# A ring of 19 half places for expert weights, and the final norm's weight spread by identity products

## The reference, cut to what matters

```python
h = h + merged @ w_out[layer]
h = h + hierarchical_moe(rmsnorm(h, norm_ffn_w[layer]), router_group_w[layer], ..., expert_w_gate[layer],
                         expert_w_up[layer], expert_w_down[layer])
out = rmsnorm(h, norm_final_w)
return out[:, N_META:]
```

## Time and profile before

| | |
|---|---|
| time, median of 3 | 776.92 us (776.09 to 777.96) |
| the profiled execution's own time | 777.54 us |
| its span | 775.8 us |
| TensorE busy (matmul) | 748.4 us, 96% |
| TensorE weight load busy | 534.8 us, 69% |
| VectorE, ScalarE, GpSimd busy | 323.0, 312.2, 124.5 us |
| moved by DMA | 241.08 MB, 311 GB/s over the span |
| granted TensorE clock, mean | 0.999 |

### The profile page before, as it was taken

The page is one execution under the profiler, slowest core; times in us unless marked ns, Lnnn a source line. Parts: engine busy times, 40 slices in busy tenths (PEclk is TensorE's granted clock), DMA queues, the critical chain, the costliest instruction groups (busy, mean ns, idle before and its releaser), DMA issues.

```text
span 775.8 us, 16103 instructions
## 1 busy us (share of the span) xinstructions
PE 748.4 (96%) x6517; PEld 534.8 (69%) x6517; DVE 323.0 (42%) x793; ACT 312.2 (40%) x632; POOL 124.5 (16%) x208
## 2 busy tenths in 40 slices
PE   8999999999999999899999999999999999998995
PEld 8989989998999988655555555565555555455452
DVE  5785787688675855812211311221222112112012
ACT  6876678576584744712112121222122121111123
POOL 7373242225433640000000000000000000000000
PEclk9999999999999999999999999999999999999999
DMA  8537555554754458999999999999999999999993
GB/s 206 145 84 179 153 139 143 138 150 111 187 141 124 144 197 307 414 408 422 412 430 427 429 427 426 427 431 424 424 429 427 427 430 426 427 427 427 422 415 125
DMA packets 83554, 241.08 MB, mean 311 GB/s; under 512 B 7185, under 2 KB 65666, under 8 KB 71826
## 3 DMA queue, kind: packets, MB, share of 16 engines
q1 hardware_dynamic: 83170, 239.19, 81.2%
q10 hardware_dynamic: 304, 0.79, 0.3%
HBM read 238.92 MB, written 1.05 MB: 309 GB/s over the span
## 4 chain that ended last, share of the span: by engine, by line
PE 72%; DMA 16%; DVE 5%; issue 3%; POOL 2%; ACT 1%; SPq 1%; DVEq 0%; POOLq 0%; ACTq 0%
PE banks L2154 22%; PE banks L1808 19%; PE banks L2212 11%; DMA ring<-in_expert_w_up_dram 10%; DMA ring<-in_expert_w_down_dram 5%; PE banks L2085 3%; PE banks L2003 2%; PE banks L2167 2%; PE banks L1927 1%; PE banks L1940 1%; PE banks L2188 1%; DVE desk L1381 1%; PE banks L1944 1%; PE banks L1965 1%; PE banks L1988 1%
## 5 line engine op out<-in xcount | busy, mean ns | idle before, releaser
L2154 PE MATMUL banks<-ring,bench 128*64 128x256 f32 x2048 | 239.9, 388 | 7.7 <-DMA ring<-in_expert_w_up_dram 5.6
L2154 PEld LDWEIGHTS banks<-ring,bench 128*64 128x64 f32 x2048 | 145.9, 134 | 108.7 <-issue 20.8
L1808 PE MATMUL banks<-rounded 128*128 128x256 f32 (+3 forms) x1344 | 197.5, 293 | 1.3 <-DVE rounded L1342 0.9
L1808 PEld LDWEIGHTS banks<-rounded 128*128 128x128 f32 (+1 forms) x1344 | 170.1, 187 | 5.3 <-POOL rounded L1206 1.1
L1711 DVE TENSOR_TENSOR bench<-banks,bench 128x256 f32<-128x256 f32 x32 | 13.6, 425 | 259.5 <-PE banks L2154 171.7
L2212 PE MATMUL banks<-ring,bench 128*64 128x512 f32 x512 | 116.9, 598 | 1.4 <-DMA ring<-in_expert_w_down_dram 0.9
L1105 ACT ACTIVATE ysb<-banks 64x512 f32<-64x512 f32 x63 | 37.3, 592 | 148.1 <-PE banks L2212 147.3
L2212 PEld LDWEIGHTS banks<-ring,bench 128*64 128x64 f32 x512 | 34.1, 136 | 64.0 <-issue 60.2
L873 ACT ACTIVATE rounded<-room 128x1024 fp32r<-128x1024 f32 x64 | 67.4, 1054 | 23.5 <-PE banks L1808 15.1
L1094 ACT ACTIVATE bench<-banks 128x256 f32<-128x256 f32 x32 | 12.3, 385 | 146.1 <-PE banks L2188 146.1
L1330 DVE TENSOR_TENSOR rounded<-room,rounded 128x1024 fp32r<-128x1024 f32 x49 | 61.4, 1252 | 16.6 <-ACT rounded L873 15.6
(11 more groups left out here) (309 smaller groups left out, 857.6 us busy)
## 6 DMA issues: line engine op xcount, KB each, us to landing
ring<-in_expert_w_down_dram SPq DMA_DIRECT2D x28, 2048.0 KB, 26.4
ring<-in_expert_w_gate_dram SPq DMA_DIRECT2D x27, 2048.0 KB, 25.2
ring<-in_expert_w_up_dram SPq DMA_DIRECT2D x27, 2048.0 KB, 26.5
room<-in_w_in_dram SPq DMA_DIRECT2D x56, 512.0 KB, 4.2
ring<-in_expert_w_up_dram SPq DMA_DIRECT2D x16, 512.0 KB, 7.0
ring<-in_expert_w_down_dram SPq DMA_DIRECT2D x16, 512.0 KB, 7.0
ring<-in_expert_w_gate_dram SPq DMA_DIRECT2D x12, 512.0 KB, 5.8
room<-in_w_out_dram SPq DMA_DIRECT2D x8, 512.0 KB, 4.3
```

The source lines that it names most:

```text
L1808: ins = T.matmul(o, a, b[:, k, lo_at:L], start=(k == 0 and n == 0), stop=(k == KT - 1 and n == 2))
L2154: ins = T.matmul(pb[5 + c][half * 64:half * 64 + SLOTS, 0:256], xgT[:, q % ROOMS, kt, j * SLOTS:(j + 1) * SLOTS], w[:, kt, half], start=(k ...
```

## The change

1. **Half places.** The ring's 9 places become 18 halves, and all of `spare` becomes a 19th (8 KB a partition each). Half h of chunk n (= 3e+c) goes to half place (2n+h) mod 19. Chunks 0 to 8 stay where they were, as whole loads. From chunk 9, gate of expert 3, each chunk is two loads of 1 MiB, with 8 KB rows: the first waits until the chunk ten before is used up, the second until half of the chunk nine before is (a new semaphore `half`, raised by TensorE in the middle of each chunk). Chunk 9's first half goes to `spare` and waits for the router's logits. `PIECES` keep their sizes. The quartered loads and their semaphore go.
2. **Landing semaphores.** There are ten (`LANDS`) in place of nine, and `landed` counts the loads of a chunk.
3. **The final norm's weight.** The 128-row load of L789 goes. In its place SyncE loads `gain_out`, 32 bytes a partition, right after `gain` at the start. In experts 28 and 29, after `turn_mid`, TensorE does `spread_gain`: 8 products each of a broadcast column of `gain_out` with 64 columns of the identity, into bank 4, and VectorE copies the bank into the new `wfin`, which lies in the second half of `xgT` of room 0 (not used after expert 27).
4. **Counts.** `gain`'s load raises `bias_land` now, so the three waits for it and for the biases become waits for all four loads. The router's count goes from 5 to 4 loads.

```diff
-ROUT = 5 * 16
+ROUT = 4 * 16
-QUARTERED = [(RINGS, 0), (RINGS, 1), (RINGS, 2), (RINGS + 1, 2)]
+HALVES = 19
+LANDS = 10
+GAIN_PARTS = 2
...
+def slot_of(e, c):
+    return (3 * e + c) % LANDS
+
+def loads_of(e, c, again):
+    if (e, c) in PIECES or e == 0 and not again:
+        return 0
+    if 3 * e + c >= HALVES // 2:
+        return 2
+    return QUARTERS if e == 1 and c < 2 and not again else 1
+
+def loads_until(e, c, again):
+    return sum(loads_of(m // 3, m % 3, again) for m in range(slot_of(e, c), 3 * e + c + 1, LANDS))
...
-        wfin = spare[:, D:2 * D]
+        gain_out = sb("gain_out", [P, KT])
...
+        wfin = xgT[:, 0, KT // 2:KT, :].rearrange("p k s -> p (k s)")
...
+        def half_at(e, c, half):
+            at = (2 * (3 * e + c) + half) % HALVES
+            if at == HALVES - 1:
+                return spare[:]
+            return ring[:, RING_AT[at // 2], at % 2 * CHUNK // 2:(at % 2 + 1) * CHUNK // 2]
...
+        def load_half(eng, e, c, half):
+            dst, src = half_at(e, c, half), (gate_v, up_v, down_v)[c][e][:, half * CHUNK // 2:(half + 1) * CHUNK // 2]
             if (e, c) in PIECES:
-                parts = PIECES[e, c]
+                parts = PIECES[e, c] // 2
...
-                eng.dma_start(dst, src).then_inc(S(f"w_land{3 * (e % RINGS) + c}"), 16)
+                eng.dma_start(dst, src).then_inc(S(f"w_land{slot_of(e, c)}"), 16)
...
-            sp.dma_start(gain[:], norm_ffn_w[0].rearrange("(p k) -> p k", k=KT)).then_inc(S("gain_land"), 16)
+            sp.dma_start(gain[:], norm_ffn_w[0].rearrange("(p k) -> p k", k=KT)).then_inc(S("bias_land"), 16)
+            sp.dma_start(gain_out[:], norm_final_w.rearrange("(p k) -> p k", k=KT)).then_inc(S("bias_land"), 16)
...
-                    taken(sp, ("G", HEADS - 1))
-                    sp.dma_start(wfin, norm_final_w[None, :].to_broadcast([P, D])).then_inc(S("rout_land"), 16)
...
                 for e in range(EXPERTS):
-                    for c, used in enumerate(("gate", "up", "y")):
-                        if (e, c) in QUARTERED and not again:
...
-                        if e >= RINGS:
-                            sp.wait_ge(S(used), base + (e - RINGS + 1))
...
+                    for c in range(3):
+                        n = 3 * e + c
+                        if 2 * n + 1 < HALVES:
+                            if again or (e and (e, c) not in EARLY):
+                                load_chunk(sp, e, c)
                             continue
+                        before = n - LANDS
+                        if before >= 0:
+                            sp.wait_ge(S(used[before % 3]), base + before // 3 + 1)
+                        elif not again:
+                            sp.wait_ge(S("logits"), TT)
+                        load_half(sp, e, c, 0)
+                        sp.wait_ge(S("half"), chunks + (before + 2))
+                        load_half(sp, e, c, 1)
...
-                    act.wait_ge(S("bias_land"), 2 * 16)
+                    act.wait_ge(S("bias_land"), 4 * 16)
...
                     if q + 1 < QUADS:
                         bring(q + 1, j)
+                    elif j < GAIN_PARTS:
+                        dve.wait_ge(S("gathered"), parts + QUADS * PARTS + j + 1)
+                        V.tensor_copy(wfin[:, j * 512:(j + 1) * 512], pb[4][:]).then_inc(S("xgT"), 1)
...
+                def spread_gain(n):
+                    pe.wait_ge(S("xgT"), parts + QUADS * PARTS + n - 2)
+                    for k in range(KT):
+                        ins = T.matmul(pb[4].rearrange("p (j k) -> p k j", k=KT)[:, k, :], gain_out[:, k:k + 1].to_broadcast([P, P]),
+                                       ident[:, n * 64:(n + 1) * 64], start=True, stop=True, skip_group_check=True)
+                    ins.then_inc(S("gathered"), 1)
...
                             ins = T.matmul(pb[5 + c][...], xgT[:, q % ROOMS, kt, j * SLOTS:(j + 1) * SLOTS],
-                                           w[:, kt, half], ...)
-                        if first and (kt + 1) % (KT // QUARTERS) == 0 and kt < KT - 1:
-                            ins.then_inc(S("quarter"), 1)
+                                           ws[kt // 4][:, kt % 4, half], ...)
+                        if kt == KT // 2 - 1:
+                            ins.then_inc(S("half"), 1)
...
                     turn_mid(e)
                     if q + 1 < QUADS:
                         gather(q + 1, j, 1)
+                    elif j < GAIN_PARTS:
+                        spread_gain(j)
```

More of the change, by code:

```diff
@@ L416, with loads_in_all @@
         LO_AT[_s[1]] = (_name, _i + 1)
-def uses(n, k, slots):
-    return (n - k + slots - 1) // slots
+def slot_of(e, c):
[8 more added lines that the diff above has]
+    return sum(loads_of(m // 3, m % 3, again) for m in range(slot_of(e, c), 3 * e + c + 1, LANDS))
+def loads_in_all(slot, again):
+    return sum(loads_of(m // 3, m % 3, again) for m in range(slot, 3 * EXPERTS, LANDS))
 def build_block(nc, x, meta_tokens, norm_mix_w, w_in, conv_w, pool_w, pool_scale, a_log, dt_bias, dn_norm_w,
@@ L1026, in _ @@
             warm(ACT.Sqrt, 2)
-            act.wait_ge(S("gain_land"), 16)
+            act.wait_ge(S("bias_land"), 4 * 16)
             def cast(n):
@@ L1652, in one_pass @@
                 again = not isinstance(ps, int)
-                experts, pairs, parts = EXPERTS * ps, PAIRS * ps, QUADS * PARTS * ps
+                experts, pairs, parts = EXPERTS * ps, PAIRS * ps, (QUADS * PARTS + GAIN_PARTS) * ps
                 def slots_of(q):
@@ L2120, in landed @@
                 def landed(e, c):
-                    short = sum(k == c and n % RINGS == e % RINGS for n, k in PIECES)
-                    if e == 0 and not again:
-                        pe.wait_ge(S(f"first_land{c}"), 4 * 16)
-                        return
-                    loads = ps * (uses(EXPERTS, e % RINGS, RINGS) - short) - (e % RINGS == 0)
-                    quarters = QUARTERS - 1 if e % RINGS == 0 or e % RINGS == 1 and (c < 2 or again or e > RINGS) else 0
-                    pe.wait_ge(S(f"w_land{3 * (e % RINGS) + c}"), 16 * (loads + quarters + (e // RINGS + 1)))
+                    loads = loads_until(e, c, again)
+                    if again:
+                        first, other = (loads_in_all(slot_of(e, c), over) for over in (False, True))
+                        loads = ps * other + (first - other + loads)
+                    pe.wait_ge(S(f"w_land{slot_of(e, c)}"), 16 * loads)
                 def gate_up(e, c, name):
@@ L2144, in gate_up @@
                             pe.wait_ge(S("give"), pairs + i)
-                    w = ring[:, RING_AT[3 * (e % RINGS) + c], :].rearrange("p (k q h j) -> p k h q j", k=KT, h=2, j=2)
+                    ws = [half_at(e, c, n).rearrange("p (k q h j) -> p k h q j", k=KT // 2, h=2, j=2) for n in range(2)]
                     for kt in range(KT):
@@ L2206, in down @@
                         landed(e, 2)
-                    w = ring[:, RING_AT[3 * (e % RINGS) + 2], :].rearrange("p (j d) -> p j d", j=4)
+                    ws = [half_at(e, 2, n).rearrange("p (j d) -> p j d", j=2) for n in range(2)]
                     for j in range(4):
```

43 lines of the change are left out of this document (17 added, 26 removed).

## The result

The changed kernel takes 780.43 us in the median of 9 runs (779.31 to 784.87), the kernel before 776.79 in 9 (775.83 to 777.96). The ratio is 1.0048, with a 95% interval of 1.0032 to 1.0064: 3.6 us slower (2.5 to 5.0). The forecast was 782.0.

A forecast was written before the change was run, and what follows sets the result against it. The full transfer queue was taken as the bound, with TensorE following it. Terms -1.3 - 0.5 - 0.3 + 6.1 + 1.1 = +5.1 us, on a median of 776.92, gave 782.0 us; range 775.9 to 785.5.

The forecast's parts named there:

- the four quartered chunks: Expert-weight chunks loaded in 512 KB quarters become 1 MiB loads, each 0.07 us faster: -0.3 us.
- What bounds the kernel: TensorE uses up its lead of loaded chunks, then follows the full transfer queue; 4.895 us per chunk, then a fixed tail.
- The halves: From chunk 9, 78 whole loads become 156 with 8 KB rows, 0.078 us more per chunk: +6.1 us, bounds 3.8 and 7.8.
- The second price: Alternative cost of halving a chunk's rows, from the slower 4 KB rows: 0.049 us per chunk instead of 0.078.
- The rival of a free row: Row length of the chunk loads costs nothing: sum -1.0, 775.9 us, the same as before; chance 0.11.
- that of a third of the price: An added row costs a third of the forecast: 78 chunks cost 2.2 us, 778.1 us, the same; chance 0.11.
- The load of `wfin`: At the start of the full queue, removing this 0.52 MB load moves all that follows up: -1.3 us, bounds -1.3 and 0.
- The gap: DMA's dip at 326 to 336 us closes as (3,0)'s first half is issued earlier: -0.5 us, bounds -1.1 and 0.
- `spread_gain`, +1.1 us: Experts 28 and 29: 3.5 us of added TensorE products less 2.4 of cover from load waits: +1.1 us, bounds 0 and 1.8.
- SyncE's queue: SyncE's doubled issues of loads, 0.43 us each, stay hidden within 4.9 us per chunk: cost 0.
- Three signs: Expected: no DMA dip at 328 us, TensorE load waits before 600 us, halves 20 to 24 us from issue to landing.
- The early waits: At the start, `gain_out` lands at about 15.8 us, before ScalarE's wait at 16.4: 0, at most +0.3 us.

The follow-up runs named there:

- two loads a chunk, 8 KB rows: The kernel before with 78 whole loads each issued as two 1 MiB loads cut by columns, ring and waits unchanged; 784.63 us, ratio 1.0094.
- Part 3 alone: The kernel before with only the final norm's weight changed (`gain_out` and `spread_gain` for the 128-row load), whole loads kept; 778.03 us, ratio 1.0008.
- the early `wfin`: The kernel before with only the 128-row load of `wfin` moved ahead of the router's loads; 776.84 us, ratio 0.9987.
- the versions with whole loads: The kernel before with `wfin` loaded earlier (0.9987), first quarter of (3,0) early (0.9988), both (0.9988), or new norm weight plus one early half (1.0008).
- the last of them: The kernel before with the new final norm's weight and the first half of (3,0) early, only once; 778.50 us, ratio 1.0008.

## Why the prediction was right

It held in direction and range: +3.6 us measured (2.5 to 5.0), +5.1 forecast. Step by step from the kernel before to the changed one, the last down product moves by 4.92 us through the halves (two loads a chunk, 8 KB rows), by -1.77 through what differs at the start of the queue (`wfin`, the gap and the four quartered chunks), and by +0.77 in the stretch behind (28,1) (48.33 against 47.56); the forecast had +6.1, -2.1 and +1.1. Each of these three is good to about 1 us. Within the middle one a term that was too large and one that was too small made up for each other, and that was luck. By its steps:

**What bounds the kernel: held up to (28,1).** The late landings moved by 3.53 us (386.87 to 390.40) and the last down product by 3.92, so the end follows the queue of loads. Cutting the loads alone slows the kernel, although TensorE has 72% of the chain. Behind (28,1) it is TensorE that sets the time in the changed kernel. One row was misread: 615.31 in the earlier trace rows is the issue of a load that lands at 653.9, and TensorE's first wait for a load late in the stage is at 639.3, so it isn't true that it waits from 615 on.

**The halves, +6.1 us: the mechanism shown, the size nearly.** Landings 14.92 us apart, as forecast, which is the forecast's 0.078 a chunk. Over the stage it's less: 73 cut chunks cost 5.30 us to (28,1), 0.073 each, and all 78 cost 4.92 to the last down product, 0.063 each. The windows of 200 us, 421 against 427 GB/s, give 0.070. The second price, 0.049 from the window of 4 KB rows, was too low: 416 GB/s there was read from a short window, and in a window of 200 us such rows move at 409. The rival of a free row, and that of a third of the price, are out.

On the page's rule: the Trainium skill, "DMA: Bandwidth & Descriptors", section "Why small descriptors are slow (HBM only)", gives a fixed cost per packet. The runs agree with that form: 8 and 24 added rows cost the same per row, as far as they can be measured. Its 3 cycles would make 2.2 us here (an estimate), and the halves cost 4.9 to 5.7 us, over twice as much.

**The load of `wfin`, -1.3 us: wrong by itself.** Part 3 alone and the early `wfin` gained nothing up to (28,1) that stands out of the 1 us of spread, and the window at the gap moves less in both. My bound of 0 named the reason, a later load that leaves the gap again.

**The gap, -0.5 us: too small, but only together.** In the changed kernel the early half is worth 1.3 us, in the landing of (28,1) and in the last down product. Against the two loads with 8 KB rows, the changed kernel lands (28,1) 392.17 - 390.40 = 1.77 us earlier, the sum of `wfin`, the gap and the four quartered chunks; I had 2.1. Two terms that I added are one: the removed load makes the queue run dry sooner, and the half fills it. In the versions with whole loads the same joint gain did not show up; only for the last of them do the rows suggest a reason, and a gain under 1 us would not show in one trace.

**`spread_gain`, +1.1 us: too much against the execution it was read from.** Its products last as forecast (1.90 us with the last one's overhang, 1.76 forecast), but the last down product moved by only 438.73 - 434.81 - 3.53 = 0.39 us more than the landings. The sum had 3.5 us of work less 2.4 of cover; in the rows it's 3.19 less 2.80. I had no cover from ScalarE's wait, and I took a wait for a load at its listed length, where its absence moves the next start by more. The larger error is in the premise: the waits of one execution were taken as fixed, and the stretch without the products differs by 1.4 us from one execution to another (47.06 to 48.50).

**SyncE's queue, 0: held.** Its issues take 2.1 us in the median, and DMA stays at 421 GB/s. From issue to landing it's 25.3 us; I had 20 to 24.

**Three signs failed.** DMA still dips, to 384 GB/s from 326 to 336 us, where I had no dip; TensorE's late waits begin at 626.5 us, not before 600; and the halves take longer from issue to landing than I had.

**The early waits, 0: not contradicted.** Nothing in the stage hangs on them; the later start of the stage in the profiled execution goes with a granted clock of 0.93.

What stays open: why a single landing comes 0.4 to 1 us late now and then, and so where the joint gain of `wfin` and the early start goes when rows stay whole. It also stays open to which term the 1.2 us belong by which the stage (+3.92) came out under the forecast: the halves are the largest part by the last down product, and by the distance of the landings they are not off at all.

## What to carry to other kernels

Where DMA is full, a finer place in a ring is paid with shorter rows: look at bytes per row and engine before looking at loads per chunk, because here about 9 ns a row decided and twice the loads cost nothing. A gap filled or a load removed at the start of a full queue counts only as far as the next issue can follow, so sum such terms jointly and not one by one. Before reading an effect of 1 us from one trace, take a second trace of the same kernel: here the landings of two executions with the same loads differed by 1.0 us. The half place that the ring gained was worth 1.3 us, at the gap; whether still more places would give anything, no run shows.

## What the runs showed of the hardware

In a full queue, each row that is added by cutting the same bytes shorter costs its DMA engine about 9 ns (427, 421 and 409 GB/s with rows of 16, 8 and 4 KB), and the number of loads costs nothing (409 GB/s with two and with four loads a chunk). A load to 64 of the 128 partitions runs at half rate, even with the other half's load queued right behind it: 221 GB/s at a DMA share of 1.01, against 427 with all 128; the fastest of its six executions, 1055.81 us, is still 36% slower than the kernel before. How far SyncE gets ahead before its issues block is not a number of bytes: at 25.3, 18.3 and 14.0 us from issue to landing some 10.7, 7.5 and 5.7 MB are on their way (an estimate from the rates), with 1 MiB loads of 8 KB rows, 1 MiB loads of 4 KB rows and 512 KB loads of 4 KB rows. Two adjacent 8 KB rows of one load, contiguous on both sides, go out as one 16 KB row (83552 packets). And the granted clock of TensorE falls in the first stage in some executions, to 0.94 to 0.81 from 60 to 80 us, with TensorE busy all of the time, and the first gate product starts up to 4 us later: the same kernel took 779.31 us at a mean clock of 0.999 and 784.87 at 0.992, more than the whole effect of the change.
